# Split products of rounded parts for values, keys and queries, and the states' reads ahead of the rotary rows

## The reference, cut to what matters

```python
z = x @ w_in                       # split into xs, gs, cq, ckv, kr, gm
ys = s5_branch(xs, ...) * silu(gs) # states, then y = gelu(y); y = y * sigmoid(y @ w_glu + b_glu)
q  = (rms_norm(cq, q_norm_g) @ w_uq)      # 1024 x 256 times 256 x 768: 4 heads of 128 plain + 64 rotary
kv = (rms_norm(ckv, kv_norm_g) @ w_ukv)   # 1024 x 128 times 128 x 1024: keys and values of 4 heads
q  = concat(q_nope, rotary(q_rope)); k = concat(k_nope, rotary(kr)); ym = softmax(q k) v * silu(gm)
mix = concat(ys, ym) @ w_out
```

## Time and profile before

| what | us |
|---|---|
| median of 3 runs | 2158.92 (2156.01 to 2160.89) |
| the profiled execution | 2164.66 |
| its span | 2162.8 |
| TensorE busy, of the span | 2079.2 |
| VectorE, GpSimd, ScalarE busy | 1357.9, 1141.4, 818.0 |
| DMA | 230.02 MB, mean 106 GB/s |

### The profile page before, as it was taken

One profiled execution on the slowest core, in us unless ns is written; L12 is line 12 of the kernel. 1 busy time (PEld: TensorE's weight loads), 2 busy tenths in 40 slices (PEclk: granted clock), 3 DMA queues, 4 the chain that ended last, 5 costly groups with the idle time before them and its releaser, 6 DMA issues.

```text
span 2162.8 us, 28447 instructions
## 1 busy us (share of the span) xinstructions
PE 2079.2 (96%) x11124; PEld 1632.0 (75%) x11124; DVE 1357.9 (63%) x1705; ACT 818.0 (38%) x1304; POOL 1141.4 (53%) x793
## 2 busy tenths in 40 slices
PE   8999989999998999999999999998999999999997
PEld 5878745878875885578857788876788888887885
DVE  7999865541768015520067424775977777778988
ACT  6232242340117005620065343134544545453443
POOL 2576713057873663346646764374677778750000
PEclk9999999999998999999999999999999999999999
DMA  7463472042232321001211325333122222137543
GB/s 298 149 142 108 115 158 77 1 185 98 88 102 81 119 78 47 28 27 52 74 24 51 113 100 202 107 117 136 35 74 88 88 88 88 64 135 283 169 152 113
DMA packets 72726, 230.02 MB, mean 106 GB/s; under 512 B 15960, under 2 KB 18824, under 8 KB 71280
## 3 DMA queue, kind: packets, MB, share of 16 engines
q1 hardware_dynamic: 59632, 170.04, 23.8%
q10 hardware_dynamic: 9104, 36.45, 4.6%
q0 software_dynamic: 3856, 21.70, 4.0%
HBM read 180.03 MB, written 46.17 MB: 105 GB/s over the span
## 4 chain that ended last, share of the span: by engine, by line
PE 74%; DVE 16%; ACT 4%; issue 2%; POOL 2%; DMA 2%; SPq 0%; ACTq 0%; DVEq 0%; POOLq 0%
PE ps L3563 22%; PE ps L3160 17%; PE ps L3678 8%; DVE back L2350 6%; PE ps L3487 4%; PE ps L3596 4%; PE ps L3634 2%; PE ps L355 2%; PE ps L3125 2%; PE ps L525 1%; PE ps L513 1%; PE ps L378 1%; PE ps L1050 1%; DMA back<-ssm_out_by_step 1%; PE ps L507 1%
## 5 line engine op out<-in xcount | busy, mean ns | idle before, releaser
L1779 POOL TENSOR_TENSOR up_parts<-front,up_parts 128x512 fp32r<-128x512 f32 x120 | 188.5, 1580 | 74.8 <-ACT up_parts L2087 74.0
L3678 PE MATMUL ps<-ffn_parts,w_parts 128*128 128x512 f32 x924 | 212.6, 392 | 5.0 <-DVE ffn_parts L2946 5.0
L3678 PEld LDWEIGHTS ps<-ffn_parts,w_parts 128*128 128x128 f32 x924 | 174.2, 189 | 42.7 <-DVE w_parts L2938 3.8
L3563 PE MATMUL ps<-t_high,up_parts 128*128 128x512 f32 x640 | 204.0, 390 | 1.2 <-ACT back L2094 0.8
L3160 PE MATMUL ps<-h_high,w_parts 128*128 128x512 f32 x672 | 187.7, 394 | 0.6 <-PE ps L3487 0.6
L1704 POOL TENSOR_TENSOR w_parts<-front,sb_zero 128x1024 fp32r<-128x1024 f32 x48 | 101.9, 2123 | 158.4 <-PE ps L3487 58.1
L3563 PE MATMUL ps<-h_high,up_parts 128*128 128x512 f32 x480 | 154.8, 389 | 0.3 <-DVE back L2755 0.2
L1709 POOL TENSOR_TENSOR w_parts<-front,w_parts 128x1024 fp32r<-128x1024 f32 x54 | 141.9, 2628 | 19.9 <-ACT w_parts L2252 7.5
L3160 PEld LDWEIGHTS ps<-h_high,w_parts 128*128 128x128 f32 x672 | 124.0, 188 | 25.8 <-issue 1.4
L3563 PEld LDWEIGHTS ps<-t_high,up_parts 128*128 128x128 f32 x640 | 120.1, 188 | 27.1 <-issue 1.5
L1590 POOL TENSOR_TENSOR front<-front,sb_csilu 128x1024 f32<-128x1024 f32 x48 | 102.6, 2137 | 61.2 <-DMA front<-w_ada 61.1
(11 more groups left out here) (445 smaller groups left out, 5039.6 us busy)
## 6 DMA issues: line engine op xcount, KB each, us to landing
front<-w_ada SPq DMA_DIRECT2D x48, 512.0 KB, 3.6
front<-w_up SPq DMA_DIRECT2D x44, 512.0 KB, 4.2
front<-w_down SPq DMA_DIRECT2D x22, 512.0 KB, 3.7
back<-w_down SPq DMA_DIRECT2D x22, 512.0 KB, 4.4
front<-w_in SPq DMA_DIRECT2D x16, 512.0 KB, 3.9
front<-w_out SPq DMA_DIRECT2D x16, 512.0 KB, 4.5
residual<-back ACTq DMA_DIRECT2D x2, 4096.0 KB, 14.9
front<-w_gates SPq DMA_DIRECT2D x16, 512.0 KB, 4.2
```

The source lines that it names most:

```text
L1779: pool.tensor_tensor(parts[:, BANK:], src, parts[:, 0:BANK].bitcast(F32), ALU.subtract)\
L3563: mm = pe.matmul(o, parts[:, at + k * P:at + (k + 1) * P], x, start=p in (1, 2, 5) and k == 0 and q == 0, stop=k == 3 and q == 2, skip_gro ...
L3678: mm = pe.matmul(ps[:, (4 if p in (2, 5, 3) else 0) + m, :], weights[:, w_ * BANK + m * P:w_ * BANK + (m + 1) * P], half_of(x, x_), start= ...
```

## The change

Weights of w_ukv and w_uq are copied on ScalarE into rounded pages (`U_HIGH`), and GpSimd writes the rest over the ring slot (`u_low`). The gain of a latent now writes a rounded page (`C_HIGH`), and VectorE writes the rest (`C_LOW`). Each product becomes three: high by high, low weight by high, high weight by low. The gains of latents 1 and 2 and the weight copies stand among the state copies. The squares no longer wait for the sums before (latent 2 has a page of its own), and the sums of latent 1 come after pass 0. On GpSimd's queue the states' reads come ahead of the rotary rows and the mask; GS waits for the keys' last tile and GM for QR1, since their pages are used until then.

```diff
@@ semaphore counts, pages
+             "c_low": ("x_low", 8), "k_low": ("x_low", 11), "q_low": ("x_low", 15),
+        U_HIGH = rounded_pages("u_weights_high", (17, 26, 27), 3)
+        C_HIGH, C_LOW = rounded_pages("latents_high", (16, 24, 25), 3), rounded_pages("latents_low", (22, 20, 21), 3)
-        TEMPS_2 = (cols(48 * PAGE + 512, 49 * PAGE + 512), page(32), page(32))
+        TEMPS_2 = (cols(48 * PAGE + 512, 49 * PAGE + 512), page(32), page(34))
@@ helpers
         def latent_square_act(act, i):
-            if i:
-                act.wait_ge(S("norm_square_used"), tiles_to("kv_norm", i))
             act.activation(TEMPS_2[i], latent(i)[0], ACT.Square).then_inc(S("norm_square"), 1)
@@ latent_gain_act
-            act.activation(x, x, ACT.Copy, scale=gain).then_inc(S("norm_ready"), 1)
+            act.activation(C_HIGH[i], x, ACT.Copy, scale=gain).then_inc(S("norm_ready"), 1)
+
+        def latent_low_dve(dve, i):
+            x, _, gain = latent(i)
+            dve.wait_ge(S("norm_ready"), tiles_to("kv_norm", i + 1))
+            dve.scalar_tensor_tensor(C_LOW[i], x, gain, C_HIGH[i].bitcast(F32), ALU.mult, ALU.subtract)\
+                .then_inc(S("c_low"), 1)
@@ gpsimd
             ada_sum(15)
+            def u_low(i):
+                raw = (B_UKV, B_UQ, B_UQ + 1)[i] % RING
+                pool.wait_ge(S("act_step"), ACT_STEP["ukv_high"] + i)
+                pool.tensor_tensor(RING_LOW[raw], ring[:, raw, :], U_HIGH[i].bitcast(F32), ALU.subtract)\
+                    .then_inc(S("pool_step"), 1)
+
+            u_low(0)
+            u_low(1)
             pool.wait_ge(S("ssm_ps_read"), 32)
             pool.dma_start(y_dram, UU).then_inc(S("y_in_dram"), 16)
+            u_low(2)
+            pool.wait_ge(S("y_in_dram"), 16)
+            for g in range(8):
+                pool.dma_start(YF[g * GC:(g + 1) * GC, :, :].rearrange("c k (s n) -> c k s n", s=STEP),
+                               y_dram.rearrange("(s c) (k g) n -> g c k s n", c=GC, g=8)[g]).then_inc(S("yf_landed"), 16)
             pool.wait_ge(S("z_free"), N_IN)
             pool.wait_ge(S("dve_step"), DVE_STEP["cm_zero"])
...
             pool.dma_start(CM[:, SEQ - P:SEQ], t["causal"]).then_inc(S("cm_landed"), 16)
-
-            pool.wait_ge(S("y_in_dram"), 16)
-            for g in range(8):
-                pool.dma_start(YF[g * GC:(g + 1) * GC, :, :].rearrange("c k (s n) -> c k s n", s=STEP),
-                               y_dram.rearrange("(s c) (k g) n -> g c k s n", c=GC, g=8)[g]).then_inc(S("yf_landed"), 16)
...
+            pool.wait_ge(*T("kv_tile", 12))
             pool.dma_start(GS, silu_dram[0:4].rearrange("k p t -> p k t")).then_inc(S("silu_back"), 16)
+            pool.wait_ge(*T("qr_tile", 2))
             pool.dma_start(GM, silu_dram[4:8].rearrange("k p t -> p k t")).then_inc(S("silu_back"), 16)
@@ scalar
+            def u_high(i):
+                b = (B_UKV, B_UQ, B_UQ + 1)[i]
+                act.wait_ge(S(f"w_landed{b % RING}"), 16 * (b // RING + 1))
+                act.activation(U_HIGH[i], ring[:, b % RING, :], ACT.Copy).then_inc(S("act_step"), 1)
+
             for x in range(24, 32):
...
+                if x == 25:
+                    u_high(0)
+                elif x == 27:
+                    latent_gain_act(act, 1)
+                    u_high(1)
+                elif x == 29:
+                    latent_gain_act(act, 2)
+                    u_high(2)
             for kt in range(8):
...
-                if kt in (3, 5):
-                    latent_gain_act(act, kt // 2)
@@ vector
             latent_dve(dve, "q_norm", (1, 2))
+            latent_low_dve(dve, 0)
...
             dve.wait_ge(S("z_tile"), 16)
+            latent_low_dve(dve, 1)
+            latent_low_dve(dve, 2)
@@ tensor
-            latent_sums_pe(pe, 1)
             pe.wait_ge(S("dve_step"), DVE_STEP["states_ready"])
...
                 if r == 0:
+                    latent_sums_pe(pe, 1)
                     latent_sums_pe(pe, 2)
...
+            pe.wait_ge(*T("c_low", 1))
+            pe.wait_ge(S("pool_step"), POOL_STEP["ukv_low"])
+            def latent_tile(bank, i, ks, at):
+                for n, (w_, x_) in enumerate(((0, 0), (1, 0), (0, 1))):
+                    for j, k in enumerate(ks):
+                        for nt in range(2):
+                            mm = pe.matmul(ps[:, bank + nt, :], u_weights[i][w_][:, at + j * BANK:at + j * BANK + P],
+                                           latents[k][x_][:, nt * BANK:(nt + 1) * BANK],
+                                           start=n == 0 and j == 0, stop=n == 2 and j == len(ks) - 1)
+                return mm
...
-                pe.matmul(ps[:, kt % 4, :], CKV[:, kt * P:(kt + 1) * P], ring[:, b % RING, BANK:2 * BANK],
-                          start=True, stop=True).then_inc(S("kv_tile"), 1)
+                for n, (w_, x_) in enumerate(((0, 0), (1, 0), (0, 1))):
+                    mm = pe.matmul(ps[:, kt % 4, :], latents[0][x_][:, kt * P:(kt + 1) * P], u_weights[0][w_][:, BANK:2 * BANK],
+                                   start=n == 0, stop=n == 2)
+                mm.then_inc(S("kv_tile"), 1)
...
```

More of the change, by code:

```diff
@@ L60 @@
              "kv_free": ("z_free", 16), "q_free": ("z_free", 28), "yg_ready": ("z_free", 32), "glu_sig": ("z_free", 36), "pp_out0": ("p_weight_landed", 16),
-             "k_low": ("x_low", 8), "q_low": ("x_low", 12),
+             "c_low": ("x_low", 8), "k_low": ("x_low", 11), "q_low": ("x_low", 15),
              "gm_high": ("win_high", 16), "x_whole": ("win_high", 20), "u_high": ("win_high", 28)}
@@ L304, in program @@
             "angle_reduced", "cm_zero", "rotary_ready"))}
-        POOL_STEP = {"w_pp_low0": 1, "w_pp_low1": 2, "w_pp_low2": 3, "tm_zero": 4, "zero": 5, "relb_ones": 10, "dist_masked": 11}
+        POOL_STEP = {"w_pp_low0": 1, "w_pp_low1": 2, "w_pp_low2": 3, "tm_zero": 4, "ukv_low": 5, "uq_low0": 6, "uq_low1": 7,
+                     "zero": 8, "relb_ones": 13, "dist_masked": 14}
         ACT_STEP = {"w_pp_high0": 1, "w_pp_high1": 2, "c_ready": 3, "dt_ready": 4, "mag_ready": 5, "sin_ready": 7,
-                    "w_pp_high2": 8, "rope_sin": 10}
+                    "w_pp_high2": 8, "ukv_high": 9, "uq_high0": 10, "uq_high1": 11, "rope_sin": 13}
         block = ctx.enter_context(nc.Block())
@@ L3301, in _ @@
                     ada_column(15, "ada_used")
-            pe.wait_ge(S("norm_ready"), tiles_to("kv_norm", 1))
-            b = B_UKV
-            block_landed(B_UKV)
+            pe.wait_ge(*T("c_low", 1))
+            pe.wait_ge(S("pool_step"), POOL_STEP["ukv_low"])
+            u_weights = [(U_HIGH[i], RING_LOW[b % RING]) for i, b in enumerate((B_UKV, B_UQ, B_UQ + 1))]
+            latents = list(zip(C_HIGH, C_LOW))
+            def latent_tile(bank, i, ks, at):
[6 more added lines that the diff above has]
+                return mm
             for kt in range(8):
@@ L3320, in _ @@
                     pe.wait_ge(*T("k_low", 1))
-                tile(K_BANK[m], b % RING, lambda k: CKV, kts=1, at=m * P).then_inc(S("kv_tile"), 1)
+                latent_tile(K_BANK[m], 0, (0,), m * P).then_inc(S("kv_tile"), 1)
             pe.wait_ge(*T("kv_tile", 12))
             pe.sem_inc(S("w_used"), 1)
-            pe.wait_ge(S("norm_ready"), tiles_to("q_norm", 2))
-            block_landed(B_UQ)
+            pe.wait_ge(*T("c_low", 3))
+            pe.wait_ge(S("pool_step"), POOL_STEP["uq_low0"])
             for m in range(4):
@@ L3333, in _ @@
                     pe.wait_ge(*T("q_low", m - 1))
-                mm = tile(2 * (m % 2), B_UQ % RING, lambda k: CQ[:, k, :], kts=2, at=m * P, step=BANK)
-                mm.then_inc(S("q_tile"), 1)
+                latent_tile(2 * (m % 2), 1, (1, 2), m * P).then_inc(S("q_tile"), 1)
             pe.wait_ge(*T("q_tile", 4))
             pe.sem_inc(S("w_used"), 1)
-            block_landed(B_UQ + 1)
+            pe.wait_ge(S("pool_step"), POOL_STEP["uq_low1"])
             for m in range(2):
@@ L3347, in _ @@
                 at = 4 - 4 * m
-                tile(at, (B_UQ + 1) % RING, lambda k: CQ[:, k, :], kts=2, at=m * P, step=BANK)
-                tile(at + 2, (B_UQ + 1) % RING, lambda k: CQ[:, k, :], kts=2, at=(2 + m) * P, step=BANK)\
-                    .then_inc(S("qr_tile"), 1)
+                latent_tile(at, 2, (1, 2), m * P)
+                latent_tile(at + 2, 2, (1, 2), (2 + m) * P).then_inc(S("qr_tile"), 1)
             pe.wait_ge(*T("qr_tile", 2))
```

## The result

| kernel | runs, median us | ratio to before, interval | profiled execution | its span |
|---|---|---|---|---|
| before | 2157.47 (6 runs) | | 2164.66 | 2162.8 |
| changed | 2167.94 (6 runs) | 1.0042, 1.0028 to 1.0055 | 2166.81 | 2165.0 |

The change costs 10.5 us, 0.42%, beyond what the measurement leaves open. I had forecast 2158.7, and 2164 as the upper end.

What follows compares the result with a forecast made beforehand. The start of the first glu tile was taken as the bound, set by the states' Gelus and QR1's end. QR1 ending at 324.2 plus glu 28.3 gave 352.5 against 352.74, so 2164.4 profiled, 2158.7 median; range 2153 to 2164.

Steps and rivals of the forecast that it cites:

- QR1: Second rotary query tile on TensorE, needing q_low 4; forecast 8.0 us, 2.5 of it for the low clock, ending at 324.2.
- The DMA wait before the Gelus: Sign in the chain of waits: this wait gone, VectorE instead waiting 10 us or more for the rotary rows, until near 308.
- the baseline: Last step of the sum: profile of before 2164.66, its runs' median 5.7 below, carried over from 2164.4 to 2158.7.
- my 352.5: Forecast end of the glu tiles on TensorE, against 352.74 before, a gain of 0.2 us; everything behind only shifts.
- the rows' landing: Rotary rows queued behind the states' reads: last read 300.9, four copies at 1.47, block 1.3, landed 308.1, before 298.9.
- The term of the weight blocks: w_glu and w_out blocks fall among reads and rows; one already counted, the other adds its 512 KB transfer, 1.3 us.
- rival 3: Weight blocks push the rotary rows back to 313.6: +5.3 us, 2164.2; decides from 312.6 on; chance 0.08.
- a queue served in order: GpSimd's DMA queue: reads land one every 2.34 us though issued every 0.68, so rotary rows queue behind them.
- What hides them: the states' passes: Preparation copies and subtractions on ScalarE, GpSimd and VectorE are covered by TensorE's states' passes, until the last state copies start, 273.2.
- The split products: On TensorE three rounded products take 0.69 us against 0.87 for a plain one; 42.0 becomes 33.0 us, 9 us less.

## Why the prediction was wrong

**The way it went was the way I had described.** The DMA wait before the Gelus is gone, VectorE waits 13.6 us for the rows, TensorE idles 12.4 us, QR1 runs mostly at the low clock and glu at the full one. Step by step, forecast and measured: write of the states issued 273.9, 272.9; reads issued 280.6, 279.8; last read 300.9, 303.6; rows 308.1, 312.36; q_low 4 316.2, 320.5; QR1 8.0 us, 8.4 and 0.4 behind it; glu 28.3, 28.2; end of glu 352.5, 357.7.

**The step that failed first is the baseline.** The runs' median came out 9.2 us above the forecast 2158.7. I wrote "the median of the runs is 2158.92, 5.7 below it, and I carry the difference over". For the profiled execution my sum says 2164.4, and the changed kernel's took 2166.81, 2.4 more; the other 6.8 us are this sentence, since the changed kernel's median lies 1.1 us above its profile and not 5.7 below. Carrying a difference over is right only if it lies where the change does nothing. The second profile of before shows a part of it in the very stretch: the reads' landing, 15.5 or 19.5 us after the last issue, and the clock that the idle of 4.65 us cost, 6.8 us in all at the end of glu, of 12.2 between the two executions. The rest lies behind glu. It may be that the changed kernel has no such short cases, since glu no longer waits for the reads; its six runs lie within 4.5 us, but no run here shows the reason. Priced against the second profile, my 352.5 would have been a loss of 6.5 us; but that execution is the fastest of its ten, so a typical baseline would have given less.

That the two profiled executions were off by only 2.4 us is in part luck. Up to the end of glu the changed kernel was 5.2 us later than I had it, and 2.7 came back behind glu, which I had said would only shift. It does not only shift: from the end of glu to the end of the program, where all the kernels here are the same, the thirteen profiles took between 1804.6 and 1813.4 us.

**Two terms of the rows' landing were too small**, by 4.3 us together. The reads, issued 0.8 us earlier than forecast, came in over 18.4 us from the first landing to the last instead of 16.4, and the first took 5.4 us instead of 3.9: 2.7 us on the last read. The term of the weight blocks, "the other adds its own transfer ... 1.3 us", held for a block that moves freely; held back itself, it moves when the rows should, and holding both blocks away gave 4.4 us. With both held, the last row landed 5.1 us behind the last read, where I had 5.9 for the four copies: that term was too large and hid a part of the miss, so that the rows behind the last read were only 1.6 us late. GS, moving beside them, was priced at nothing and has an unknown share. The outcome is close to rival 3 (chance 0.08), without reaching it: it puts the rows at 313.6 and decides from 312.6, they landed at 312.3, and the blocks cost 4.4 of its 6.8 us.

**The reason for the queueing was wrong in one point.** I called it "a queue served in order", on the landings 2.34 us apart. The copies on ScalarE's queue waited just as long, so it is not the order of one queue that puts them behind the reads. This changes no number above, but it changes the remedy: another queue does nothing, an earlier request does. The Trainium skill, "DMA: Bandwidth & Descriptors", section on queues, rings and completion order, has an engine go round-robin between queue rows by packets. I took from it, as an estimate, that copies on a second queue would be through in about twice their lone time; with 21.6 us, no packet of q10 for 10 us and 17 of q1 to 282 of q0, the trace does not agree. What keeps the others back, no run here shows.

**The preparation was costed at its lone durations.** "What hides them: the states' passes" held for TensorE's first value tile, but not for VectorE: beside GpSimd's subtractions three of its instructions took 3.4, 2.9 and 3.4 us in the changed kernel where 1.2, 0.7 and 0.7 are the lone durations (1.28, 0.69 and 0.70 in the kernel without these subtractions). The fourth key tile waited 4.9 us, and the first rotary query tile ended at 308.0, not 302.9. In the changed kernel the wait for the rows covers this; once the rows are early it is the next bound, worth 3.6 us in the runs (2154.34 to 2150.76; 3.0 against before beside each), with VectorE's order put back at the same time.

**The split products** were priced right by themselves: 24 value products in 5.66 us, 0.23 each, and about 3 us of run time once the order let them count, in so far as the intervals allow. With the reads behind the rows they brought an idle, and 5 us in the runs that no profile explains.

## What to carry to other kernels

A transfer that fills the DMA engines and is moved ahead can push back what is requested after it, whatever the queue; ask first what small transfer somebody waits for, and let that one go ahead of the big one, to another buffer if its own is not free yet. Profile a kernel twice before trusting the difference between a profile and the median: if the chain runs through a DMA, the difference may sit exactly where the change is, or far behind it; here it was 6.8 and 5.4 us. And a faster engine ahead of an unchanged wait earns an idle, behind which two glu tiles here took 1.7 to 2.6 us longer.

## What was not expected of the hardware

Requests on three different queues (GpSimd's, the sync engine's, ScalarE's) made while the eight reads, cut by 16 partitions, were under way took 15 to 22 us, where the rotary copies of before took 3.0 to 5.8 and a w_glu block 3.4; cut by time step, the same reads let a w_glu block through in 7.7 to 8.6. And beside a 128x1024 tensor_tensor on GpSimd three of VectorE's instructions took 2.1 to 3.3 us longer than without it: a scalar_tensor_tensor 1.28 and 3.41, a cast 0.69 and 3.99, a tensor_scalar 0.70 and 3.08. Not every instruction pays: in the profile with the long ones two scalings of VectorE, from 263.2 us, took 1.2 us each beside a sum on GpSimd.
